# Four RMS norms that spread their sums with one product, in a two-block transformer kernel

## The chip, the cores and the metric

The kernel runs on one core of a Trainium2 chip, in one launch. The metric is the time of one execution in microseconds (us) of the device; the time before is the median of three runs. Engines are named as in the profile: PE is TensorE's products, PEld its weight loads, DVE is VectorE, ACT ScalarE, POOL GpSimd, SP SyncE (which issues the loads of weights).

## The reference

512 tokens of width 1024 pass a first block (two layers: a mixer, then cross attention to a memory of 256 rows) and a second block (pooling, latent attention, memory attention, a gated merge, then a mixture of 32 experts). What matters here are the norms:

```python
def rmsnorm(x, g):
    xf = x.astype(jnp.float32)
    y = xf * lax.rsqrt(jnp.mean(xf * xf, axis=-1, keepdims=True) + EPS)
    return (y * g.astype(jnp.float32)).astype(x.dtype)
...
        x = x + memory_cross_attention(rmsnorm(x, c_norm[i]), rmsnorm(mem, c_mem_norm[i]),
                                       c_wq[i], c_wkv[i], c_wo[i])
    return rmsnorm(x, final_norm)
```

Both layers of the first block norm the same `mem`, with different gains. The first block ends with a norm (gain `final_norm`), and the second begins with another one on its result (`mix_norm_g`), so two norms follow each other directly.

## The kernel before, in words

Activations lie transposed: features on the 128 partitions in 8 tiles (`KT`), the 512 tokens along the free dimension (`T`). A norm therefore sums over partitions and tiles. Every weight product is made in fp32r from high and low parts: `three` (with `tile`, 24 products for one output tile of 8 x 3) multiplies high by high, high by low, low by high. Weights come in units of 128x1024 through a ring of three buffers: SP loads one, ACT makes its high part (L572, `highs_through`, due once the unit three before it has been used), POOL its low part (L537). Output tiles go round four PSUM banks `G`; a bank is free again once DVE has emptied it (`evac`). Each engine runs a list written out by hand, in the order of the code; waits are semaphores.

The norm's factor is applied after the product: the inputs carry only the gain, and DVE multiplies each emptied tile by `RB`, the inverse root of each token's mean square, the same on all partitions (`scaled`, L1027). A norm runs so: ACT squares each tile (`norm_tile`, L585) and makes its high part (L587), DVE makes the low part (L988) and adds the squares up in `sumsq` (L993, L996). Then PE sums over the partitions with four column products of `sumsq` against a column of ones (`norm_cols`, into `O[:, 0:4]`: tokens on partitions now). ACT takes the root (`norm_root`, L592), DVE inverts it (`norm_cols` of DVE, L1003) and scales four 128x128 identity pieces with it (L1005, into `sq`), PE multiplies ones by this diagonal (`norm_bc`, into `TR`, the value of every token on all partitions), and DVE copies it to `RB` (`norm_bc` of DVE, L1014).

The norms in order: "e", "m0" (memory, 256 columns), "c0", "o", "m1" (memory again), "c1", "fm", "kvd", "qd", "m2", "ffn", "f2". Those the change touches:

- "c0" and "c1" (`cross`): columns after the third k tile, spreading after the fifth. `RB` is used from the q tiles on, which come after eight k tiles and the v tiles.
- "o": columns after the first conv tile, spreading after the second.
- "m1": squares and sums of the memory tiles on ACT and DVE (`mem_norm`, `mem_tiles`), columns and spreading inside the projection `o_out` (`project` with `beside`, `residual` with `beside`). Until `RBm` is there, the residual's own tiles are held back.
- "fm", the last norm of the first block and the first of the second in one: two sums are kept (`sumsq` of x squared and `sumsq_f`, of x times the gain squared). Eight columns after tile kvd0; a root (L765), an inverse `rcf` (L1359), the second sum scaled by it (L1360, L1361), a second root (L767) and inverse (L1363, L1364); two diagonals (L1366, L1368), two spreading products after tile kvd1, two copies (L1374 to `RB`, L1375 to `RBf`).

After "fm" DVE goes on in this order: `scaled` kvd0 and kvd1 with their norm tiles, `cosq` and `sinq` (L1381, L1382), `norm_cols` of "kvd", the rotation of kr (L1053, L1056, L1388), `scaled` qd0, the copy of RBk, qd1 and qd2 with their norm tiles. PE's order is kvd0, kvd1, kr, qd0, columns of "kvd", qd1, spreading of "kvd", qd2, uv0, columns of "qd", uk0, spreading of "qd". ACT makes the high part of the next unit between its norm tiles (`unit_done`).

Of the kernel before, what the change touches and what calls it, by code (L numbers as in the profile page):

```python
# [110 lines left out]
def build(nc, stream, x_in, mem_in, mem2_in, vectors, tables, decay, window, causal, pool_edge, positions, ident_in,  # L111
          router_w, router_b, iota_in, slot_in, before_in, w_gu, w_dn, out):
    ctx = ExitStack()
    with ctx:
# [25 lines left out]
        rcf = sb("rcf", [P, 4])  # L140
        rcq = sb("rcq", [P, 4])
        fm_ss = sb("fm_ss", [P, 4])
# [9 lines left out]
        sb("line_b", [P, HALF_LINE])  # L152
# [142 lines left out]
        NB, BC = {}, {}  # L295
        tiles = splits = 0
        for i, (name, n, w, split) in enumerate(NORMS):
            NB[name] = (i, tiles, splits, n, w, split)
            BC[name] = i - (1 if name == "f2" else 0)
            tiles += n  # L300
            splits += split

# [50 lines left out]
        sumsq_f, diag_f = U[:, 7, :], U[:, 6, :]  # L353
# [206 lines left out]
        def _(act):  # L560
# [17 lines left out]
            def norm_tile(name, f, src, gain, dst, ready):  # L578
                i, base, sbase, n, w, split = NB[name]
                act.wait_ge(*ready)  # L580
                if base + f >= 2:
                    act.wait_ge(ssq, base + f - 1)
                if f == 0 and i > 0:
                    act.wait_ge(bc_full, BC[name])
                nc.scalar.activation(sq[:, (base + f) % 2, 0:w], src, ACT.Square).then_inc(xsq, 1)  # L585
                if split:
                    nc.scalar.activation(dst, src, ACT.Identity, scale=gain).then_inc(xhi, 1)  # L587

            def norm_root(name, width):
                i, _, _, n, w, _ = NB[name]  # L590
# [100 lines left out]
            def mem_norm(name, raw, landed_sem, gain, beside):  # L691
# [4 lines left out]
                norm_root(name, D)  # L696
                unit_done(beside, 2)
                act.wait_ge(rb_ready, NB[name][0] + 1)
# [39 lines left out]
            norm_root("o", D)  # L738
# [12 lines left out]
            i, tile0 = NB["fm"][0], NB["fm"][1]  # L751
            for f in range(KT):
# [5 lines left out]
                if f == 0:  # L758
                    act.wait_ge(bc_full, i)
# [4 lines left out]
            act.wait_ge(col_full, i + 1)  # L764
# [175 lines left out]
            def final(again, added):  # L940
                i, base = NB["f2"][0], NB["f2"][1] - 1 + again * SUMMED
# [7 lines left out]
                act.wait_ge(col_full, i + 1 + again)  # L949
# [18 lines left out]
        def _(dve):  # L968
# [15 lines left out]
            def norm_tile(name, f, src, gain, hi, lo):  # L984
                i, base, sbase, n, w, split = NB[name]
                if split:
                    dve.wait_ge(xhi, sbase + f + 1)
                    nc.vector.scalar_tensor_tensor(lo, src, gain, hi, ALU.mult, ALU.subtract).then_inc(xlo, 1)  # L988
                dve.wait_ge(xsq, base + f + 1)
                if f == 0:  # L990
                    if i:
                        dve.wait_ge(col_full, i)
# [6 lines left out]
            def norm_cols(name, dst):  # L999

                i, _, _, n, w, _ = NB[name]
                dve.wait_ge(col_root, i + 1)
# [8 lines left out]
            def norm_bc(name, dst):  # L1011
                i, w = BC[name], NB[name][4]
                dve.wait_ge(bc_full, i + 1)
                nc.vector.tensor_copy(dst[:, 0:w], TR[:, 0:w]).then_inc(rb_ready, 1)  # L1014
                dve.wait_ge(rb_ready, i + 1)

# [297 lines left out]
            norm_end("o", rc, RB)  # L1314
# [19 lines left out]
            residual("o_out", "c1", "c_norm1", beside="m1")  # L1334
# [5 lines left out]
            i, tile0, split0 = NB["fm"][0:3]  # L1340
            for f in range(KT):
# [6 lines left out]
                for e, total in enumerate((sumsq[:, :], sumsq_f)):  # L1348
                    dve.wait_ge(xsq, tile0 + 2 * f + e + 1)
                    if f == 0:  # L1350
                        if e == 0:
                            dve.wait_ge(col_full, i)
# [9 lines left out]
            dve.wait_ge(col_root, i + 1)  # L1362
            do(nc.vector.reciprocal(rc[:, :], root[:, :]))  # L1363
            do(nc.vector.tensor_tensor(rc[:, :], rc[:, :], rcf[:, :], ALU.mult))  # L1364
            for t in range(TT):
                note(nc.vector.tensor_scalar(sq[:, 0, t * P:(t + 1) * P], ident[:, :], rc[:, t:t + 1], None, ALU.mult))  # L1366
            for t in range(TT):
                ins = nc.vector.tensor_scalar(diag_f[:, t * P:(t + 1) * P], ident[:, :], rcf[:, t:t + 1], None,  # L1368
                                              ALU.mult)
                if t < TT - 1:  # L1370
                    note(ins)
            ins.then_inc(diag, 1)
            dve.wait_ge(bc_full, i + 1)
            note(nc.vector.tensor_copy(RB[:, :], TR[:, :]))  # L1374
# [1289 lines left out]
```

## Time and profile before

| what | value |
|---|---|
| median of 3 runs | 1624.59 us (1622.58 to 1625.92) |
| profiled execution | 1624.31 us |
| its span, first to last instruction | 1622.5 us |
| PE busy | 1584.3 us, 98% of the span, 7432 products |
| PEld, DVE, ACT, POOL busy | 1203.4, 840.6, 583.8, 547.1 us |
| granted TensorE clock, mean | 0.991 of full speed |

The page gives, for one execution, each engine's busy time; the chain that ended last, followed back from the last instruction; and groups of instructions with the idle time ahead of them. The trace can be asked for the instructions of a stretch in order of time. In such an answer a line has the start in us from the span's start, the duration, engine, line, operation, out<-in, shape and count; a group that is merged begins at its first. Matmuls are pipelined: their starts tell the pace, their durations overlap. A product in fp32 (not fp32r) is issued as two.

### The profile page before, as it was taken

To read this page: it belongs to the slowest core of one execution; us is meant where nothing else is said; L and a number is where in the kernel's file an instruction comes from. 1 tells how busy PE (TensorE), PEld (TensorE's weight loads), DVE (VectorE), ACT (ScalarE), POOL (GpSimd) and SP (SyncE) were. 2 spreads that over 40 slices of the span, in tenths; PEclk is the share of its full clock that TensorE was granted. 3 is DMA by queue.
4 is the path that set the end of the run, shared out by engine and by line. 5 is a ranking of instruction groups with operands and counts; after the bars stand their busy time and mean duration, and the time that the engine had idled before them with its cause. 6 is when DMAs were issued, how large, how long until landed. Compare 5 with 4: busy or idle time off the path is not lost.

```text
span 1622.5 us, 20099 instructions
## 1 busy us (share of the span) xinstructions
PE 1584.3 (98%) x7432; PEld 1203.4 (74%) x7432; DVE 840.6 (52%) x1456; ACT 583.8 (36%) x963; POOL 547.1 (34%) x239
## 2 busy tenths in 40 slices
PE   7999989999999999999999999999999999999997
PEld 5888769886888888987887767888877885444543
DVE  6447586135645557354668686344243644433434
ACT  4127454334322225325533343343243333112213
POOL 4441226731444444851433124455424410000000
PEclk9999999999999999999999999999999989999998
DMA  5331224522223233531223013334312449999991
GB/s 188 96 99 40 78 78 130 163 85 71 92 91 101 95 96 99 168 118 41 79 78 91 27 52 97 100 125 128 97 52 92 153 179 368 417 423 422 421 418 68
DMA packets 52787, 235.94 MB, mean 145 GB/s; under 512 B 6240, under 2 KB 7136, under 8 KB 48096
## 3 DMA queue, kind: packets, MB, share of 16 engines
q1 hardware_dynamic: 48960, 222.60, 38.9%
q0 software_dynamic: 2016, 7.34, 1.1%
q10 hardware_dynamic: 1728, 4.87, 0.9%
q8 instruction: 55, 0.90, 0.2%
q14 instruction: 28, 0.23, 0.0%
HBM read 230.59 MB, written 4.19 MB: 145 GB/s over the span
## 4 chain that ended last, share of the span: by engine, by line
PE 90%; DVE 5%; ACT 2%; issue 1%; DMA 0%; SPq 0%; DVEq 0%; ACTq 0%
PE G L1804 69%; PE O L1804 7%; PE S L1804 6%; PE TR L1804 4%; PE TR L1914 2%; PE G L2376 1%; DVE sq L1056 1%; DMA w_ring<-in_stream_dram 0%; ACT hi_ring L572 0%; DVE U L1027 0%; DVE arena L1205 0%; DVE sumsq L1126 0%; DVE arena L1200 0%; DVE arena L1426 0%; DVE U L1781 0%
## 5 line engine op out<-in xcount | busy, mean ns | idle before, releaser
L537 POOL TENSOR_TENSOR lo_ring<-w_ring,hi_ring 128x1024 fp32r<-128x1024 f32 x219 | 533.4, 2437 | 775.2 <-ACT hi_ring L572 774.8
L572 ACT ACTIVATE hi_ring<-w_ring 128x1024 fp32r<-128x1024 f32 x219 | 231.2, 1058 | 577.8 <-PE G L1804 573.7
L1804 PE MATMUL G<-xa_hi,hi_ring 128*128 128x512 f32 x928 | 375.6, 405 | 9.8 <-DVE xa_lo L1118 9.6
L1804 PE MATMUL G<-xa_hi,lo_ring 128*128 128x512 f32 x928 | 362.4, 391 | 0.0
L1804 PE MATMUL G<-xa_lo,hi_ring 128*128 128x512 f32 x928 | 362.1, 390 | 0.0
L1804 PEld LDWEIGHTS G<-xa_hi,hi_ring 128*128 128x128 f32 x928 | 174.9, 188 | 48.2 <-issue 12.2
L1804 PEld LDWEIGHTS G<-xa_lo,hi_ring 128*128 128x128 f32 x928 | 174.9, 188 | 38.0 <-issue 2.6
L1804 PEld LDWEIGHTS G<-xa_hi,lo_ring 128*128 128x128 f32 x928 | 174.6, 188 | 37.1
L1804 PE MATMUL G<-yb_hi,hi_ring 128*128 128x512 f32 x388 | 153.4, 395 | 4.1 <-ACT arena L670 2.2
L1804 PE MATMUL G<-yb_hi,lo_ring 128*128 128x512 f32 x388 | 151.1, 389 | 0.0
L1804 PE MATMUL G<-yb_lo,hi_ring 128*128 128x512 f32 x388 | 151.0, 389 | 0.0
L1027 DVE TENSOR_TENSOR arena<-G,RB 128x512 f32<-128x512 f32 x77 | 52.6, 689 | 156.4 <-PE G L1804 155.8
L548 POOL DMA_INDIRECT ex_raw<-token_rows,arena x14 | 13.3, 947 | 227.0 <-DVE arena L1676 224.8
L1804 PEld LDWEIGHTS G<-yb_hi,hi_ring 128*128 128x128 f32 x388 | 72.8, 188 | 20.6 <-issue 5.2
L1804 PEld LDWEIGHTS G<-yb_lo,hi_ring 128*128 128x128 f32 x388 | 72.8, 188 | 15.9 <-issue 1.0
L1804 PEld LDWEIGHTS G<-yb_hi,lo_ring 128*128 128x128 f32 x388 | 72.8, 188 | 15.3
L1804 PE MATMUL G<-cm_hi,hi_ring 128*128 128x256 f32 (+1 forms) x212 | 69.3, 327 | 0.1
L996 DVE TENSOR_TENSOR sumsq<-sumsq,sq 128x512 f32<-128x512 f32 (+1 forms) x51 | 65.6, 1286 | 1.9 <-ACT sq L585 1.9
L1804 PE MATMUL G<-cm_hi,lo_ring 128*128 128x256 f32 (+1 forms) x212 | 65.6, 309 | 0.0
L1804 PE MATMUL G<-cm_lo,hi_ring 128*128 128x256 f32 (+1 forms) x212 | 65.6, 309 | 0.0
L1804 PE MATMUL G<-ex_rings,U 128*64 128x512 f32 x160 | 57.9, 595 | 0.0
L1804 PE MATMUL TR<-ex_rings,U 128*64 128x512 f32 x128 | 56.6, 595 | 0.0
(350 smaller groups left out, 2503.0 us busy)
## 6 DMA issues: line engine op xcount, KB each, us to landing
w_ring<-in_stream_dram SPq DMA_DIRECT2D x219, 512.0 KB, 3.5
arena<-in_w_gu_dram SPq DMA_DIRECT2D x16, 2048.0 KB, 11.5
ex_rings<-in_w_dn_dram SPq DMA_DIRECT2D x40, 512.0 KB, 15.2
ex_low<-in_w_gu_dram SPq DMA_DIRECT2D x8, 2048.0 KB, 17.8
ex_rings<-in_w_gu_dram SPq DMA_DIRECT2D x8, 2048.0 KB, 15.4
arena<-in_w_dn_dram SPq DMA_DIRECT2D x16, 512.0 KB, 13.7
sq<-in_w_dn_dram SPq DMA_DIRECT2D x8, 512.0 KB, 17.3
X<-in_x_in_dram SPq DMA_DIRECT2D x8, 256.0 KB, 5.8
```

The source lines that it names most:

```text
L537: nc.gpsimd.tensor_tensor(lo_ring[:, s, :], w_ring[:, s, :], hi_ring[:, s, :], ALU.subtract).then_inc(low, 1)
L548: nc.gpsimd.indirect_dma_start(slot_rows[p], None, token_rows, where).then_inc(rows_land[p], 16)
L572: nc.scalar.activation(hi_ring[:, m % RING, :], w_ring[:, m % RING, :], ACT.Copy).then_inc(high, 1)
L996: nc.vector.tensor_tensor(sumsq[:, 0:w], sumsq[:, 0:w], sq[:, (base + f) % 2, 0:w], ALU.add).then_inc(ssq, 1)
L1027: nc.vector.tensor_tensor(dst, G[:, a % BANKS, 0:w], by, ALU.mult).then_inc(evac, done)
L1056: ins = nc.vector.tensor_tensor(part[other, 1, :], bank[r, :], sin[r, :], ALU.mult)
L1804: return nc.tensor.matmul(*args, **kw)
L1914: ins = nc.tensor.transpose(TR[:, b * P:(b + 1) * P], prob(probs, u, b * P, (b + 1) * P), ident[:, :])
L2376: ins = nc.tensor.transpose(G[:, f // 2, c:c + P], slot_rows[p][:, f * P:(f + 1) * P], ident[:, :])
```

## The change

The norms "c0", "o", "c1" and "fm" are marked `wide`: one product of ones (128x128) with `sumsq` (128x512) puts each token's sum on all partitions at once, ACT takes the root of 128x512, and DVE inverts it in place. Columns, diagonal and the copy fall away for them. In "c0" and "c1" the product stands where the columns stood, after the third k tile; in "o" after the first conv tile; in "fm" two products stand after tile kvd0, where the columns stood, and none after kvd1. "m1" has no squares, sums, columns or spreading: `rcm` and `RBm` of "m0" are used again, since the memory is the same. The semaphore counts are kept in tables of their own (`COL`, `BC`, `ROOT`, `DIAG`, `SUMS_READ`), since not every norm signals each of them any more.

```diff
@@ the norms @@
-        NORMS = [("e", KT, T, KT), ("m0", KT, MEM, KT), ("c0", KT, T, KT), ("o", KT, T, KT), ("m1", KT, MEM, KT),
-                 ("c1", KT, T, KT), ("fm", 2 * KT, T, KT), ("kvd", 2, T, 2), ("qd", 3, T, 3),
-                 ("m2", KT, MEM, KT), ("ffn", KT, T, 0), ("f2", KT, T, 0)]
+        NORMS = [("e", KT, T, KT, "cols"), ("m0", KT, MEM, KT, "cols"), ("c0", KT, T, KT, "wide"),
+                 ("o", KT, T, KT, "wide"), ("m1", 0, MEM, KT, ""), ("c1", KT, T, KT, "wide"),
+                 ("fm", 2 * KT, T, KT, "wide"), ("kvd", 2, T, 2, "cols"), ("qd", 3, T, 3, "cols"),
+                 ("m2", KT, MEM, KT, "cols"), ("ffn", KT, T, 0, "cols only"), ("f2", KT, T, 0, "cols")]
@@ tiles @@
-        rcf = sb("rcf", [P, 4])
-        fm_ss = sb("fm_ss", [P, 4])
-        sb("line_b", [P, HALF_LINE])
+        sb("line_b", [P, HALF_LINE + 8])
@@ ACT @@
+            def wide_root(name):
+                act.wait_ge(bc_full, BC[name] + 1)
+                nc.scalar.activation(RB[:, :], TR[:, :], ACT.Sqrt, bias=eps[:, :], scale=1.0 / D).then_inc(col_root, 1)
...
                         if name[0] == "k" and j == 2:
-                            norm_root(norm, D)
+                            wide_root(norm)
...
             residual("o0", "o", "o_norm")
-            norm_root("o", D)
+            wide_root("o")
...
             unit_done("kvd", 0)
-            act.wait_ge(col_full, i + 1)
-            nc.scalar.activation(root[:, :], O[:, 0:4], ACT.Sqrt, bias=eps[:, :], scale=1.0 / D).then_inc(fm_root, 1)
+            act.wait_ge(bc_full, BC["fm"] + 1)
+            nc.scalar.activation(RBf, TR[:, :], ACT.Sqrt, bias=eps[:, :], scale=1.0 / D).then_inc(fm_root, 1)
             act.wait_ge(fm_mid, 1)
-            nc.scalar.activation(root[:, :], fm_ss[:, :], ACT.Sqrt, bias=eps[:, :], scale=1.0 / D).then_inc(col_root, 1)
+            nc.scalar.activation(RB[:, :], RB[:, :], ACT.Sqrt, bias=eps[:, :], scale=1.0 / D).then_inc(col_root, 1)
             unit_done("kvd", 1)
@@ DVE @@
+            def wide_inverse(name):
+                dve.wait_ge(col_root, ROOT[name] + 1)
+                nc.vector.reciprocal(RB[:, :], RB[:, :]).then_inc(rb_ready, 1)
+                dve.wait_ge(rb_ready, BC[name] + 1)
...
             def cross(i, norm):
                 for j in range(KT):
                     scaled(ACC0[f"k{i}"] + j, xk[:, j, :], RBm[:, :], MEM)
-                    if j == 3:
-                        norm_cols(norm, rc)
                     if j == 4:
-                        norm_bc(norm, RB)
+                        wide_inverse(norm)
...
             residual("o0", "o", "o_norm")
-            norm_end("o", rc, RB)
+            wide_inverse("o")
...
-            residual("o_out", "c1", "c_norm1", beside="m1")
+            residual("o_out", "c1", "c_norm1")
...
             dve.wait_ge(fm_root, 1)
-            do(nc.vector.reciprocal(rcf[:, :], root[:, :]))
-            do(nc.vector.tensor_tensor(fm_ss[:, :], O[:, 4:8], rcf[:, :], ALU.mult))
-            nc.vector.tensor_tensor(fm_ss[:, :], fm_ss[:, :], rcf[:, :], ALU.mult).then_inc(fm_mid, 1)
-            dve.wait_ge(col_root, i + 1)
-            do(nc.vector.reciprocal(rc[:, :], root[:, :]))
-            do(nc.vector.tensor_tensor(rc[:, :], rc[:, :], rcf[:, :], ALU.mult))
...
-            note(nc.vector.tensor_copy(RB[:, :], TR[:, :]))
-            nc.vector.tensor_copy(RBf, O[:, :]).then_inc(rb_ready, 1)
-            settle()
-            dve.wait_ge(rb_ready, i + 1)
+            do(nc.vector.reciprocal(RBf, RBf))
+            do(nc.vector.tensor_tensor(RB[:, :], O[:, :], RBf, ALU.mult))
+            nc.vector.tensor_tensor(RB[:, :], RB[:, :], RBf, ALU.mult).then_inc(fm_mid, 1)
+            dve.wait_ge(col_root, ROOT["fm"] + 1)
+            do(nc.vector.reciprocal(RB[:, :], RB[:, :]))
+            nc.vector.tensor_tensor(RB[:, :], RB[:, :], RBf, ALU.mult).then_inc(rb_ready, 1)
+            dve.wait_ge(rb_ready, BC["fm"] + 1)
@@ PE @@
-            def norm(name):
-                norm_cols(name)
-                norm_bc(name)
+            def norm_wide(name):
+                base, _, n, _, _ = NB[name]
+                pe.wait_ge(ssq, base + n)
+                mm(TR[:, :], ones[:, :], sumsq[:, :], start=True, stop=True).then_inc(bc_full, 1)
...
                     if j == 2:
-                        norm_cols(norm_name)
-                    if j == 4:
-                        norm_bc(norm_name)
+                        norm_wide(norm_name)
...
             tile("conv", 0, xa_hi, xa_lo, ready=low_ready("o"))
-            norm_cols("o")
-            tile("conv", 1, xa_hi, xa_lo)
-            norm_bc("o")
-            for i in range(2, 32):
+            norm_wide("o")
+            for i in range(1, 32):
                 tile("conv", i, xa_hi, xa_lo)
-            project("o_out", yb_hi, yb_lo, YL["conv"], y_low, KT - 1, beside="m1")
+            project("o_out", yb_hi, yb_lo, YL["conv"], y_low, KT - 1)
...
             tile("kvd", 0, xa_hi, xa_lo, ready=low_ready("fm"))
-            i, tile0 = NB["fm"][0], NB["fm"][1]
-            pe.wait_ge(ssq, tile0 + 2 * KT)
-            for e, total in enumerate((sumsq[:, :], sumsq_f)):
-                for t in range(TT):
-                    ins = mm(O[:, 4 * e + t:4 * e + t + 1], total[:, t * P:(t + 1) * P], ones[:, 0:1],
-                             start=True, stop=True)
-            ins.then_inc(col_full, 1)
+            pe.wait_ge(ssq, NB["fm"][0] + 2 * KT)
+            mm(TR[:, :], ones[:, :], sumsq[:, :], start=True, stop=True)
+            mm(O[:, :], ones[:, :], sumsq_f, start=True, stop=True).then_inc(bc_full, 1)
             tile("kvd", 1, xa_hi, xa_lo)
-            pe.wait_ge(diag, i + 1)
-            mm(TR[:, :], ones[:, :], sq[:, 0, :], start=True, stop=True)
-            mm(O[:, :], ones[:, :], diag_f, start=True, stop=True).then_inc(bc_full, 1)
             tile("kr", 0, xa_hi, xa_lo)
```

Squares and sums of a norm are skipped where its count of tiles is 0 ("m1"), on ACT and DVE alike; ACT's `mem_norm` then neither takes a root nor waits for `rb_ready`.

## Rows read from the trace of the kernel before

**Rows 1.** The page: PE's busy time, and the chain that ended last by engine.

```profile
PE 1584.3 (98%) x7432; PEld 1203.4 (74%) x7432; DVE 840.6 (52%) x1456; ACT 583.8 (36%) x963; POOL 547.1 (34%) x239
...
PE 90%; DVE 5%; ACT 2%; issue 1%; DMA 0%; SPq 0%; DVEq 0%; ACTq 0%
```

**Rows 2.** Busy us by stretch: PE, PEld, DVE, ACT, POOL; PEclk, DMA share, GB/s.

```profile
1280.00:1622.00 342.00, 328.17 (x1618) 184.97 (x1616) 150.89 (x295) 89.31 (x142) 25.38 (x19) 0.96 0.82 333
```

**Rows 3.** The chain that ended last from 800 to 870: start, us, what.

```profile
799.94 17.91 PE G L1804 x79
...
827.07 10.94 PE G L1804 x48
838.10 1.06 ACT hi_ring L572
...
856.64 0.69 DVE sumsq L996
857.37 1.05 PE O L1804 x8
```

**Rows 4.** PE in order of time around norm "o".

```profile
432.16 0.95 PE L1804 MATMUL O<-ones,sumsq 128*128 128x1 f32 x8
...
438.53 1.02 PE L1804 MATMUL TR<-sq,ones 128*128 128x512 f32 x2
```

**Rows 5.** PE in order of time around norm "m1".

```profile
618.96 0.50 PE L1804 MATMUL O<-ones,sumsq 128*128 128x1 f32 x4
...
624.91 0.59 PE L1804 MATMUL TR<-sq,ones 128*128 128x256 f32 x2
...
625.81 0.40 PE L1804 MATMUL G<-yb_hi,lo_ring 128*128 128x512 f32 x1
```

**Rows 6.** PE in order of time around norm "fm" and the kvd columns.

```profile
817.85 1.05 PE L1804 MATMUL O<-ones,sumsq 128*128 128x1 f32 x8
...
825.19 1.02 PE L1804 MATMUL TR<-sq,ones 128*128 128x512 f32 x2
...
837.84 0.95 PE L1804 MATMUL O<-ones,sumsq 128*128 128x1 f32 x8
```

**Rows 7.** A root over 128x512 (durations min/median/max) and two reciprocals in a row.

```profile
L670 ACT ACTIVATE arena<-G,eps x2: 687/687/687, 188.3 to 212.3; 128x512 f32<-128x512 f32 x2
...
213.03 3.37 DVE L1200 RECIPROCAL arena<-arena 128x256 f32<-128x256 f32 x2 [1.31 <-ACT arena L670]
```

**Rows 8.** ACT and DVE in order of time in and after norm "fm".

```profile
820.31 0.27 ACT L765 ACTIVATE root<-O,eps 128x4 f32<-128x4 f32 x1
...
822.26 0.87 DVE L1366 TENSOR_SCALAR sq<-ident,rc 128x128 f32<-128x128 f32 x4
...
827.72 0.68 DVE L1375 COPY arena<-O 128x512 f32<-128x512 f32 x1
828.49 0.69 DVE L1027 TENSOR_TENSOR U<-G,RB 128x512 f32<-128x512 f32 x1
...
834.76 2.89 DVE L1381 TENSOR_TENSOR arena<-arena,RB 128x512 f32<-128x512 f32 x1
837.58 0.68 DVE L1382 TENSOR_TENSOR arena<-arena,RB 128x512 f32<-128x512 f32 x1
839.41 0.18 DVE L1003 RECIPROCAL rck<-root 128x4 f32<-128x4 f32 x1 [1.15 <-ACT root L592]
839.62 2.69 DVE L1005 TENSOR_SCALAR sq<-ident,rck 128x128 f32<-128x128 f32 x4
```

**Rows 9.** POOL and DVE in order of time: ops that meet each other.

```profile
630.97 5.43 POOL L537 TENSOR_TENSOR lo_ring<-w_ring,hi_ring 128x1024 fp32r<-128x1024 f32 x2 [7.78 <-ACT hi_ring L572]
...
634.07 2.88 DVE L996 TENSOR_TENSOR sumsq<-sumsq,sq 128x512 f32<-128x512 f32 x1
...
834.49 2.62 POOL L537 TENSOR_TENSOR lo_ring<-w_ring,hi_ring 128x1024 fp32r<-128x1024 f32 x1 [5.51 <-ACT hi_ring L572]
839.24 2.40 POOL L537 TENSOR_TENSOR lo_ring<-w_ring,hi_ring 128x1024 fp32r<-128x1024 f32 x1 [2.13 <-ACT hi_ring L572]
```

More of the change, by code:

```diff
@@ L289, in build @@
         stored = sem("out_stored")
-        NORMS = [("e", KT, T, KT), ("m0", KT, MEM, KT), ("c0", KT, T, KT), ("o", KT, T, KT), ("m1", KT, MEM, KT),
-                 ("c1", KT, T, KT), ("fm", 2 * KT, T, KT), ("kvd", 2, T, 2), ("qd", 3, T, 3),
-                 ("m2", KT, MEM, KT), ("ffn", KT, T, 0), ("f2", KT, T, 0)]
[L295 to L299, printed above, removed]
+        NORMS = [("e", KT, T, KT, "cols"), ("m0", KT, MEM, KT, "cols"), ("c0", KT, T, KT, "wide"),
+                 ("o", KT, T, KT, "wide"), ("m1", 0, MEM, KT, ""), ("c1", KT, T, KT, "wide"),
+                 ("fm", 2 * KT, T, KT, "wide"), ("kvd", 2, T, 2, "cols"), ("qd", 3, T, 3, "cols"),
+                 ("m2", KT, MEM, KT, "cols"), ("ffn", KT, T, 0, "cols only"), ("f2", KT, T, 0, "cols")]
+        NB, COL, BC, ROOT, DIAG, SUMS_READ = {}, {}, {}, {}, {}, {}
+        tiles = splits = cols = bcs = roots = diags = 0
+        before_it = None
+        for name, n, w, split, kind in NORMS:
+            NB[name] = (tiles, splits, n, w, split)
+            COL[name], BC[name], ROOT[name], DIAG[name] = cols, bcs, roots, diags
+            SUMS_READ[name] = before_it
             tiles += n
             splits += split
+            if kind:
+                cols += kind != "wide"
+                bcs += kind != "cols only"
+                diags += kind == "cols"
+                roots += 1
+                before_it = (bc_full, bcs) if kind == "wide" else (col_full, cols)
         YB = {}
@@ L352, in build @@
         RBf = A(4224, T)
-        sumsq_f, diag_f = U[:, 7, :], U[:, 6, :]
+        sumsq_f = U[:, 7, :]
         qrope = A(4992, 2, T)
@@ L578, in norm_tile @@
             def norm_tile(name, f, src, gain, dst, ready):
-                i, base, sbase, n, w, split = NB[name]
+                base, sbase, n, w, split = NB[name]
                 act.wait_ge(*ready)
[L581 to L585, printed above, removed]
+                if n:
+                    if base + f >= 2:
+                        act.wait_ge(ssq, base + f - 1)
+                    if f == 0 and BC[name]:
+                        act.wait_ge(bc_full, BC[name])
+                    nc.scalar.activation(sq[:, (base + f) % 2, 0:w], src, ACT.Square).then_inc(xsq, 1)
                 if split:
@@ L695, in mem_norm @@
                 unit_done(beside, 1)
-                norm_root(name, D)
+                if NB[name][2]:
+                    norm_root(name, D)
                 unit_done(beside, 2)
-                act.wait_ge(rb_ready, NB[name][0] + 1)
+                if NB[name][2]:
+                    act.wait_ge(rb_ready, BC[name] + 1)
             def residual(stage, norm, gain, split=True):
@@ L940, in final @@
             def final(again, added):
-                i, base = NB["f2"][0], NB["f2"][1] - 1 + again * SUMMED
+                base = NB["f2"][0] - 1 + again * SUMMED
                 for f in range(KT):
@@ L948, in final @@
                     nc.scalar.activation(sq[:, f % 2, :], X[:, f, :], ACT.Square).then_inc(xsq, 1)
-                act.wait_ge(col_full, i + 1 + again)
+                act.wait_ge(col_full, COL["f2"] + 1 + again)
                 nc.scalar.activation(root[:, :], O[:, 0:4], ACT.Sqrt, bias=eps[:, :],
@@ L988, in norm_tile @@
                     nc.vector.scalar_tensor_tensor(lo, src, gain, hi, ALU.mult, ALU.subtract).then_inc(xlo, 1)
+                if not n:
+                    return
                 dve.wait_ge(xsq, base + f + 1)
                 if f == 0:
-                    if i:
-                        dve.wait_ge(col_full, i)
+                    if SUMS_READ[name]:
+                        dve.wait_ge(*SUMS_READ[name])
                     nc.vector.tensor_copy(sumsq[:, 0:w], sq[:, (base + f) % 2, 0:w]).then_inc(ssq, 1)
@@ L1011, in norm_bc @@
             def norm_bc(name, dst):
-                i, w = BC[name], NB[name][4]
+                i, w = BC[name], NB[name][3]
                 dve.wait_ge(bc_full, i + 1)
@@ L1702, in square_sum @@
             def square_sum(again, f):
-                base = NB["f2"][1] - 1 + again * SUMMED
-                dve.wait_ge(xsq, NB["f2"][1] + again * KT + f + 1)
+                base = NB["f2"][0] - 1 + again * SUMMED
+                dve.wait_ge(xsq, NB["f2"][0] + again * KT + f + 1)
                 if f == 0:
-                    dve.wait_ge(col_full, NB["f2"][0] + again)
+                    dve.wait_ge(col_full, COL["f2"] + again)
                     nc.vector.tensor_copy(sumsq[:, :], sq[:, 0, :]).then_inc(ssq, 1)
@@ L1771, in final @@
             def final(again):
-                i = NB["f2"][0]
-                dve.wait_ge(col_root, i + 1 + again)
+                dve.wait_ge(col_root, ROOT["f2"] + 1 + again)
                 do(nc.vector.reciprocal(rc[:, :], root[:, :]))
@@ L1888, in norm_cols @@
             def norm_cols(name):
-                i, base, _, n, w, _ = NB[name]
+                base, _, n, w, _ = NB[name]
                 pe.wait_ge(ssq, base + n)
@@ L2115, in _ @@
             base = SU["mla"]
-            pe.wait_ge(rb_ready, NB["kvd"][0] + 1)
+            pe.wait_ge(rb_ready, BC["kvd"] + 1)
             wide("uv0", 1, TT, lat_hi, lat_lo, 3, 2)
@@ L2227, in _ @@
                 tile("xq", j, xa_hi, xa_lo)
-            pe.wait_ge(rb_ready, NB["m2"][0] + 1)
+            pe.wait_ge(rb_ready, BC["m2"] + 1)
             base = SU["x2"]
@@ L2294, in _ @@
             pe.wait_ge(raw_up, 4)
-            base = NB["ffn"][1]
+            base = NB["ffn"][0]
             for part in range(2):
@@ L2466, in final @@
             def final(again):
-                base = NB["f2"][1]
+                base = NB["f2"][0]
                 def columns(part, first, last):
```

37 lines of the change are left out of this document (14 added, 23 removed).

## The prediction, made before the change was run

> **What bounds the kernel now.** I read the page first: TensorE (PE) is busy for 98% of the span and carries 90% of the chain that ended last [rows 1]. A shorter PE program is therefore a shorter kernel, unless another engine's chain takes over. The last 340 us move 333 GB/s with the DMA engines busy for 82% [rows 2]; its loads start on events that PE's own progress sets, so time saved before it passes through whole.
>
> Then I read the chain of waits around the double norm "fm", a stretch in which PE does not set the pace alone. 79 products take 17.91 us, a pace of 0.2267 us each, and 48 more run without a break up to about 838; but from 838.10 to 857.37 the chain is ACT and VectorE (DVE), and PE waits at its end for the last sum of "qd" [rows 3]. So a saving on PE ahead of 838 counts only as far as this DVE chain comes earlier too.
>
> **The change, part by part.** The times are those of the trace of before; what is saved upstream moves all of them alike.
>
> PE, norms "c0", "c1" and "o": four column products each go. In "o" they start at 432.16, and after the 24 products of one tile the spreading product starts at 438.53 [rows 4]: 6.37 less 24 x 0.2267 (5.44) leaves 0.93 us. "c0" and "c1" issue the same four, 0.93 each. The spreading product itself stays: it has the same shape, ones as weights and 512 columns moving, and only sits where the columns were.
>
> PE, norm "m1": two columns (618.96 to 624.91 less 5.44: 0.51) and the spreading product of 256 columns (the third product after it starts at 625.81 instead of 625.36: 0.45) go: 0.96 [rows 5].
>
> PE, "fm": eight columns and two spreading products become two spreading products. Columns: 825.19 less 817.85 less 5.44 is 1.90. The pair: 837.84 less 825.19 less 48 x 0.2267 (10.88) is 1.77, so 0.89 for one [rows 6]. The pair now comes right behind tile kvd0 at 817.85, and qd0 ends at 817.85 + 1.77 + 72 x 0.2267 = 835.94 instead of 837.84.
>
> So PE alone loses 3 x 0.93 + 0.96 = 3.75 us outside "fm" and 1.90 in it, 5.65 together.
>
> DVE and ACT, "c0", "c1", "o": a root over 128x512 for one over 128x4 (0.69 against 0.27 us [rows 7, 8]), and a reciprocal over 128x512 for a small one, four diagonal pieces and a copy. Two reciprocals over 128x256 in a row take 3.37 [rows 7], so I take 3.36 for one over 128x512; the fixed part of a second instruction, at most the 0.18 of a reciprocal of 4 columns [rows 8], could go, and nothing in the trace runs longer per column. I cost all this at nothing. What hides it: in "c0" and "c1" RB is first read by the q tiles, after the v tiles, and four PSUM banks let the next k tile be emptied some 1 us late. If that cover were gone, PE would stop for about that 1 us. In "o" RB is ready at about 432.16 + 1.02 + 0.69 + 3.36 = 437.3, where the old spreading product only starts at 438.53 [rows 4]. The product there still waits for the same sum as the columns did.
>
> "m1": eight squares on ACT and eight sums on DVE go; ACT no longer waits for RBm before the residual. PE waits for none of them now, so nothing comes back, and rcm and RBm of "m0" are simply kept. The 8 floats by which line_b grows make up for rcf and fm_ss. No DMA or queue moves.
>
> **The chain in "fm"** is what decides. New, in order:
> 1. The pair of products ends at 817.85 + 0.86 + 1.02 = 819.73. ACT's table load ends at 820.31, where the old root starts [rows 8]. Root over 128x512 from PSUM, 0.69 [rows 7]: 821.0.
> 2. DVE: reciprocal 3.36 (824.4), product with a PSUM operand 0.69 (825.1), product from SBUF 0.68 (825.8); GpSimd (POOL) is idle then.
> 3. ACT: second root, by the same row at most 0.69: 826.5. Only then can ACT convert the weights of the tile that kvd1 freed, 1.06 us, and POOL's op of 2.40 [rows 9] runs from about 827.55 to 829.95.
> 4. DVE: second reciprocal to 829.9, then the last product, which meets the end of that POOL op: about 830.6. Before, the two copies ended at 828.4 and the first scaled tile began at 828.49 [rows 8]. RB comes 2.15 late, and PE runs 1.90 early.
>
> From there the scaling, the latent norms and their sums shift by 2.15. PE, which reaches the kvd columns at 835.94, waits for the kvd sum until 837.0. The product cosq, 2.89 long at 834.76, is shown beside a POOL op of 2.62 at 834.49 and should be beside it again [rows 8, 9]. But the second ACT conversion now needs no wait (qd0 is long done), so the next POOL op is queued right behind the first. The trace has that case: two POOL ops back to back take 5.43 from 630.97, one DVE op gets in between them, and the DVE product started at 634.07 takes 2.88 [rows 9]. So sinq, 0.68 before [rows 8], waits out the second POOL op: that ends at 836.64 + 5.43 + 0.2 = 842.3, and sinq at 842.85. Reciprocal and four diagonal pieces (0.87 without POOL, 2.69 beside it [rows 8]) follow: 843.95 instead of 842.31. Everything that DVE does up to the last qd sum comes 1.65 late, so PE passes 857.37 at 859.0. It loses the 1.90 and 1.65 more.
>
> What that weighs by rule: the Trainium skill, SBUF — State Buffer, section "SBUF: two separate sides", says that DVE ops with two SBUF inputs and GpSimd ops take a shared port pair as an exclusive lock, and the one that starts first blocks the other for its whole length. By it sinq waits as above. A rule that speaks against the sizes here: the Trainium skill, VectorE: DVE Perf Modes, section "First, the fixed hardware budget", gives the reciprocal a repeat count of 8, which with that page's clock of 0.96 GHz would be an estimate of 4.27 us for 512 columns. The trace disagrees: two of 256 take 3.37 [rows 7]. By it the sum would be -0.3 instead of -2.1.
>
> **Sum.** -3.75 + 1.65 = -2.1 us. The profiled execution took 1624.31 (span 1622.5 and 1.8 around it), so 1622.2; it lies 0.28 below the median of the three runs, 1624.59, from which the same difference gives 1622.5. I say 1622.4.
>
> **Rivals.** What a measurement of this kernel can tell from no change is about 0.2%, 3.25 us.
> - **Sinq gets in first.** If DVE keeps its turn between the two POOL ops, the diagonal ends at about 842.4 and "fm" costs 0.1: -3.65, 1620.7. For: it takes only a few tenths more between two ops of POOL. Against: the pair at 630.97 [rows 9]. Chance 0.23.
> - **"fm" hidden whole.** If PE had slack for all of the longer chain, the full 5.65 shows: 1618.7. For: three tiles, 16.3 us, lie between the pair and the kvd columns. Against: the chain from 838.10 is already without slack [rows 3]. Chance 0.08.
> - **One more collision.** The last product of step 4 starts at the very end of a POOL op; should that op begin a little later (ACT's conversion is tied to step 3), it takes 2.9 instead of 0.7, and "fm" costs 3.85: +0.1, 1624.4. The change then saves nothing, against what its text says. Two reciprocals that are 0.9 us longer each than their row says would end near the same place (-0.3); [rows 7] speaks against it. Chance for both, 0.14. (The second is what the Trainium skill's page VectorE: DVE Perf Modes, section "First, the fixed hardware budget", would give.)
> - **Slower: the long reciprocal holds POOL.** Place: k4 of "c0" and "c1", and "fm". If a reciprocal of 3.36 shut POOL out, the weights' low parts, one 2.40 op for each 2.88 us of a k tile, would come up to 2.9 late against some 1.9 us of slack: 1.1 each. In "fm" the same lock puts the POOL op behind the second reciprocal and the last product behind it: 3.85. That is -3.75 + 2.2 + 3.85 = +2.3, 1626.6. It decides as soon as POOL's ops wait longer than the ring's slack. Against: the reciprocal at 839.41 takes its usual 0.18 in the middle of a POOL op, where the diagonal behind it is held [rows 8]. No row shows the large one beside POOL. Chance 0.07.
>
> My forecast has 0.48. Range: 1619.6 to 1625.6 leaves out the hidden case and the slower one, and allows about 1 us beyond the two nearer rivals for the runs' own spread. Faster by over 0.2% needs 3.25 us: the hidden case, two thirds of the first rival and some 0.07 of my own tail, 0.30. Slower by over 0.2% takes a slower case that comes out worse, 0.05. Within: 0.65.
>
> **What would show it.** Right: 22 column products and one spreading product fewer; RECIPROCAL 128x512 five times at 3.3 to 3.4 us; a PE wait of about 1 us before the kvd columns and of some tenths before the kvd spreading product; sinq at 2.9; the stretch from kvd0's end to the qd columns (39.52 us before) at about 41.2. Wrong: that stretch under 40 us (first or second rival), a last "fm" product of over 2 us (third), POOL ops stretched to over 3 us in the k tiles (fourth), or a PE wait in c0, c1 or o that was not there.

## The result, and the profile after

The changed kernel takes 1643.62 us (median of 4 runs, 1642.60 to 1643.78), the kernel before 1624.79 beside it: a ratio of 1.0115, with a 95% interval of 1.0102 to 1.0128. That is 19 us slower, where the prediction said 2 us faster and its range ended at 1625.6. The profiled execution has a span of 1641.8 us against 1622.5.

The page of the changed kernel, busy time and chain; [rows 1] are the same lines of before:

```profile
PE 1599.0 (97%) x7386; PEld 1196.3 (73%) x7386; DVE 852.0 (52%) x1419; ACT 583.0 (36%) x954; POOL 547.3 (33%) x239
...
PE 89%; DVE 7%; issue 2%; ACT 2%; DMA 0%; SPq 0%; DVEq 0%; ACTq 0%
```

PE issues 46 products fewer (the 22 columns and one spreading product of the forecast, each issued as two) and is busy 14.7 us longer. The same page's groups of weight products (count, then busy us and mean ns of one) say which:

```profile
L1810 PE MATMUL G<-xa_hi,hi_ring 128*128 128x512 f32 x928 | 380.7, 410 | 9.3 <-DVE xa_lo L1139 9.3
L1810 PE MATMUL G<-xa_lo,hi_ring 128*128 128x512 f32 x928 | 367.5, 396 | 0.0
...
L1810 PE MATMUL G<-yb_hi,lo_ring 128*128 128x512 f32 x388 | 151.7, 391 | 0.0
```

And the same groups on the page of before:

```profile
L1804 PE MATMUL G<-xa_hi,hi_ring 128*128 128x512 f32 x928 | 375.6, 405 | 9.8 <-DVE xa_lo L1118 9.6
...
L1804 PE MATMUL G<-xa_lo,hi_ring 128*128 128x512 f32 x928 | 362.1, 390 | 0.0
...
L1804 PE MATMUL G<-yb_hi,lo_ring 128*128 128x512 f32 x388 | 151.1, 389 | 0.0
```

`xa` is the normed input of a projection, `yb` the result of a mixer or of attention on its way into the next projection, and `cm` the normed memory and later the latents; each is a tile pair of high and low parts. The 2784 products with `xa` as the input have become slower, though no instruction among them was touched; those with `yb` as the input, with weights from the same rings, hardly. A product's duration is modelled, so I read the pace, that is, the time from one product's start to the next, in a stretch that holds nothing but such products. Of three products that follow each other one is high weights by `xa_lo`; its group from 500 to 600 us, in the kernel before and in the changed one (count, min/median/max ns, first and last start):

```profile
L1804 PE MATMUL G<-xa_lo,hi_ring x147: 389/389/389, 500.2 to 599.5; 128*128 128x512 f32 x147
```

```profile
L1810 PE MATMUL G<-xa_lo,hi_ring x144: 393/395/397, 499.7 to 599.8; 128*128 128x512 f32 x144
```

Before, 99.3 us for 146 steps of three: 0.2267 us for a product. After, 100.1 for 143: 0.2333. Every single one in this stretch is slow (least 393 ns, where the most before was 389), so it is no wait here and there. Taken over all 928 steps, that is an estimate of 928 x (0.7000 - 0.6801) = 18.4 us. The products with `cm` as the input went both ways: by their groups' busy time 2.5 us more for those of 512 columns, 2.0 less for those of 256. Where the ring is the moving operand and `cm` or `xa` lies in the array, the groups gained 1.8 and 0.5 us.

The wide products, PE in order of time (in brackets the idle time ahead and what ended it):

```profile
274.69 1.12 PE L1810 MATMUL TR<-sumsq,ones 128*128 128x512 f32 x2 [1.44 <-DVE sumsq L1012]
...
437.73 1.02 PE L1810 MATMUL TR<-sumsq,ones 128*128 128x512 f32 x2
...
665.72 1.13 PE L1810 MATMUL TR<-sumsq,ones 128*128 128x512 f32 x2 [1.43 <-DVE sumsq L1012]
...
828.50 1.12 PE L1810 MATMUL TR<-sumsq,ones 128*128 128x512 f32 x2
...
869.67 1.05 PE L1810 MATMUL O<-ones,sumsq 128*128 128x1 f32 x8 [1.13 <-DVE sumsq L1012]
```

In "c0" and "c1" PE waits 1.44 and 1.43 us for the last sum, which it did not before. So the account is 18.4 + 2.9 of waits - 2.1 of the forecast = 19.2, against 19.3 between the two spans. It names the two large terms; that it meets the difference to a tenth is luck. Its first term is read from 100 us (by busy time the three `xa` groups gained 15.4), and the smaller changes of the other groups are left out.

**"fm" itself went as forecast.** The chain that ended last in the changed kernel, behind the end of kvd0:

```profile
831.12 0.70 ACT arena L779
...
831.84 3.36 DVE arena L1378
...
835.23 0.70 DVE RB L1379
...
835.96 0.70 DVE RB L1380
...
836.68 0.73 ACT RB L781
...
837.44 3.36 DVE RB L1382
...
840.82 0.70 DVE RB L1383
```

and DVE and POOL behind it in order of time, to be held against [rows 8, 9]:

```profile
847.55 5.40 POOL L544 TENSOR_TENSOR lo_ring<-w_ring,hi_ring 128x1024 fp32r<-128x1024 f32 x2 [6.73 <-ACT hi_ring L579]
847.82 2.87 DVE L1388 TENSOR_TENSOR arena<-arena,RB 128x512 f32<-128x512 f32 x1
...
850.62 2.88 DVE L1389 TENSOR_TENSOR arena<-arena,RB 128x512 f32<-128x512 f32 x1
...
853.75 0.87 DVE L1021 TENSOR_SCALAR sq<-ident,rck 128x128 f32<-128x128 f32 x4
```

Two reciprocals of 3.36, the last product 0.70 without a collision, two POOL ops back to back, `sinq` at 2.88, the diagonal without POOL at 0.87. From 828.50 to 869.67 is 41.17 us, where the prediction named about 41.2. All of that is right, and it weighs 2 us in a kernel that lost 19.

What did move is where the tiles lie in SBUF. Tiles are laid one behind the other in the order of their declaration. The offsets below are those of the two built programs, not of a trace. In them each small tile takes 32 bytes of a partition, although `rcf` and `fm_ss` need 16. Two of them go (64 bytes), `line_b` grows by 32, and the tiles behind it lie 32 bytes lower:

```
byte offset in a partition    before     changed
xa_hi                          32896       32896
xa_lo                          49280       49280
hi_ring                       171392      171360
lo_ring                       183680      183648
yb_lo                         195968      195936
yb_hi                         212352      212320
```

The weights (rings) and `yb` moved together; `xa` and `cm` stayed. That fits which products became slow, and was the theory for the runs.

### The profile page after: what moved, and what is told of

The parts are those of the page before. It is cut to its first block, busy times and chain, and to the rows that moved or that the text cites. A ratio compares the mean times of both kernels' runs of the same rounds, so it can differ in the third digit from the quotient of the medians.

```text
span 1641.8 us, 19943 instructions
## 1 busy us (share of the span) xinstructions
PE 1599.0 (97%) x7386; PEld 1196.3 (73%) x7386; DVE 852.0 (52%) x1419; ACT 583.0 (36%) x954; POOL 547.3 (33%) x239
## 4 chain that ended last, share of the span: by engine, by line
PE 89%; DVE 7%; issue 2%; ACT 2%; DMA 0%; SPq 0%; DVEq 0%; ACTq 0%
PE G L1810 69%; PE O L1810 7%; PE S L1810 6%; PE TR L1810 4%; PE TR L1921 2%; DVE sumsq L1012 1%; PE G L2372 1%; DVE sq L1077 1%; DVE U L1048 0%; DMA w_ring<-in_stream_dram 0%; ACT hi_ring L579 0%; DVE sumsq L1147 0%; DVE arena L1433 0%; DVE U L1787 0%; DVE arena L1226 0%
## 5 line engine op out<-in xcount | busy, mean ns | idle before, releaser
L1810 PE MATMUL G<-xa_hi,hi_ring 128*128 128x512 f32 x928 | 380.7, 410 | 9.3 <-DVE xa_lo L1139 9.3
L1810 PE MATMUL G<-xa_lo,hi_ring 128*128 128x512 f32 x928 | 367.5, 396 | 0.0
L1810 PE MATMUL G<-xa_hi,lo_ring 128*128 128x512 f32 x928 | 367.3, 396 | 0.0
```

The costliest lines, as they stand in the source:

```text
L1810: return nc.tensor.matmul(*args, **kw)
```

## The experiments

### The changed kernel with the rings put back

```diff
-        sb("line_b", [P, HALF_LINE + 8])
+        sb("line_b", [P, HALF_LINE + 16])
```

> The changed kernel whole, with line_b eight floats longer still, so that the three weight rings and the two yb tiles lie at the byte offsets of the kernel before (w_ring at 159104 in place of 159072). No instruction differs from the changed kernel. Placement theory (the 19 us are TensorE's pace: products whose weights come from a ring moved by 32 bytes and whose inputs did not move take 0.234 us in place of 0.227): the median gap of xa products returns to 0.227 us, and the time is the blind forecast's sum, 1624.6 - 2.1 = 1622.5 us, with a stretch from kvd0's end to qd's columns of some 41.2 us. Rival (the new instructions themselves slow TensorE: the wide products, the long reciprocals, another order of the two engines' access to SBUF): the gap stays at 0.234 and the time at 1643 to 1644 us.

Measured: 1624.2 us (11 runs) against 1626.06 for the kernel before on the same chip (23 runs), ratio 0.9994 [0.9985, 1.0002], that is 1.0 us faster with an interval of -2.4 to +0.3. (Here and below the ratio with its interval is not the quotient of the two medians; those are 1.9 us apart.) The pace is back, 100.0 us for 147 steps, 0.2268:

```profile
L1810 PE MATMUL G<-xa_lo,hi_ring x148: 389/389/389, 500.0 to 600.0; 128*128 128x512 f32 x148
```

Eight floats that nothing reads are worth 1.2% of this kernel; the instructions of the change are not what slowed it. Since the placement is now the one of before, its trace can be laid beside that one term by term. PE at the sums of c0, o, c1 and fm, at the kvd columns and at the qd columns:

```profile
271.49 1.02 PE L1810 MATMUL TR<-sumsq,ones 128*128 128x512 f32 x2
...
432.95 1.02 PE L1810 MATMUL TR<-sumsq,ones 128*128 128x512 f32 x2
...
654.61 1.02 PE L1810 MATMUL TR<-sumsq,ones 128*128 128x512 f32 x2
...
815.80 1.12 PE L1810 MATMUL TR<-sumsq,ones 128*128 128x512 f32 x2
...
835.20 1.02 PE L1810 MATMUL O<-ones,sumsq 128*128 128x1 f32 x8 [1.07 <-DVE sumsq L1012]
...
856.79 1.05 PE L1810 MATMUL O<-ones,sumsq 128*128 128x1 f32 x8 [1.14 <-DVE sumsq L1012]
```

The columns of c0 and c1 in the kernel before (those of o and fm are in [rows 4, 6]):

```profile
269.81 0.95 PE L1804 MATMUL O<-ones,sumsq 128*128 128x1 f32 x8
...
655.78 0.95 PE L1804 MATMUL O<-ones,sumsq 128*128 128x1 f32 x8
```

From c0's sum to o's: 162.35 before, 161.46 here, so c0's term is 0.89. From o to c1: 223.62 and 221.66, 1.96 for o and m1. From c1 to fm: 162.07 and 161.19, 0.88. Together 3.73, forecast 3.75. From fm to the qd columns: 39.52 and 40.99, a loss of 1.47, forecast 1.65; PE's wait ahead of the kvd columns, 1.07, is the one forecast at about 1 us. The waits of 1.44 and 1.43 ahead of c0 and c1 are gone. By these stretches the change saves 3.73 - 1.47 = 2.26 us. The two spans (1622.5 and 1619.1) lie further apart; the rest arises ahead of c0 and behind the qd columns, where nothing was changed.

### The kernel before with the rings moved as in the changed one

```diff
-        sb("line_b", [P, HALF_LINE])
+        sb("line_b", [P, HALF_LINE - 8])
```

> The kernel before with nothing changed but line_b, eight floats shorter, so that the rings and the yb tiles lie 32 bytes lower, as in the changed kernel. Placement theory: the gap of xa and cm products goes from 0.227 to 0.234 us, that of yb products stays, and the time rises by 19 to 22 us to 1644 to 1646 us. Rival (the new instructions): 1624.6 us, as before.

Measured: 1646.67 us (4 runs), ratio 1.0134 [1.0119, 1.0149], 21.8 us slower (20.6 between the medians). `xa` at 0.2333 us (99.4 for 142 steps), `yb` unchanged (27.9 us for 41 steps, 0.2268), and PE waits before c0's and c1's columns, though no wide sum is there:

```profile
L1804 PE MATMUL G<-xa_lo,hi_ring x143: 393/395/397, 500.2 to 599.6; 128*128 128x512 f32 x143
...
L1804 PE MATMUL G<-yb_lo,hi_ring x42: 389/389/390, 395.6 to 423.5; 128*128 128x512 f32 x42
...
274.68 1.05 PE L1804 MATMUL O<-ones,sumsq 128*128 128x1 f32 x8 [1.43 <-DVE sumsq L996]
...
668.51 1.05 PE L1804 MATMUL O<-ones,sumsq 128*128 128x1 f32 x8 [1.44 <-DVE sumsq L996]
```

18.4 + 2.9 is 21.3, and its span is 1643.9, 21.4 over the one of before; the same reserve holds as for the first account. So these two waits come with the placement as well. What they come from shows in "c0". The last sum on DVE in the kernel before, which began together with a POOL op at 268.33:

```profile
268.33 0.68 DVE L996 TENSOR_TENSOR sumsq<-sumsq,sq 128x512 f32<-128x512 f32 x1
```

and the same sum in the changed kernel, behind a POOL op that began 0.09 us earlier:

```profile
271.69 2.39 POOL L544 TENSOR_TENSOR lo_ring<-w_ring,hi_ring 128x1024 fp32r<-128x1024 f32 x1 [0.39 <-ACT hi_ring L579]
271.78 2.86 DVE L1012 TENSOR_TENSOR sumsq<-sumsq,sq 128x512 f32<-128x512 f32 x1
```

In "c1" it is the same (654.29 and 0.68 before, 662.81 and 2.85 after). That the slower pace is what shifts the two engines against each other is read from the traces; no run here changed the shift alone.

### The changed kernel with "fm" as it was, at the placement of before

```diff
-                 ("fm", 2 * KT, T, KT, "wide"), ("kvd", 2, T, 2, "cols"), ("qd", 3, T, 3, "cols"),
+                 ("fm", 2 * KT, T, KT, "fm"), ("kvd", 2, T, 2, "cols"), ("qd", 3, T, 3, "cols"),
...
+        rcf = sb("rcf", [P, 4])
+        fm_ss = sb("fm_ss", [P, 4])
...
-        sb("line_b", [P, HALF_LINE + 8])
+        sb("line_b", [P, HALF_LINE])
...
-            mm(TR[:, :], ones[:, :], sumsq[:, :], start=True, stop=True)
-            mm(O[:, :], ones[:, :], sumsq_f, start=True, stop=True).then_inc(bc_full, 1)
+            for e, total in enumerate((sumsq[:, :], sumsq_f)):
+                for t in range(TT):
+                    ins = mm(O[:, 4 * e + t:4 * e + t + 1], total[:, t * P:(t + 1) * P], ones[:, 0:1],
+                             start=True, stop=True)
+            ins.then_inc(col_full, 1)
```

(and the roots, inverses, diagonals and copies of the kernel before on ACT and DVE).

> The changed kernel with the norm fm put back as it was (columns, diagonals, rcf and fm_ss), so four wide sums are down to three, and with every tile at its address of before. Forecast's terms: c0, c1, o and m1 save 0.93 x 3 + 0.96 = 3.75 us of TensorE and fm costs nothing: 1624.6 - 3.75 = 1620.9 us, 1.65 under the changed kernel at the same placement. Rival A (c0's wide sum waits for VectorE, as it did for 1.2 us in the changed kernel): 1622.0 us. Rival B (fm's new chain costs nothing, so its products' saving stands): this kernel is 1.9 us slower than the changed kernel at the same placement.

Measured: 1622.93 us, the median of 11 runs, ratio 0.9981 [0.9972, 0.9990] to the kernel before: 3.1 us faster, -4.5 to -1.6. A twelfth run took 4139.96 us; it is left out, and its cause stays open (with it the median is 1623.34). This kernel is faster than the one before, clear of noise. PE at the sums of o and c1, at fm's columns and at the qd columns:

```profile
436.00 1.02 PE L1824 MATMUL TR<-sumsq,ones 128*128 128x512 f32 x2
...
657.70 1.02 PE L1824 MATMUL TR<-sumsq,ones 128*128 128x512 f32 x2
...
818.89 1.05 PE L1824 MATMUL O<-ones,sumsq 128*128 128x1 f32 x8
...
858.42 1.05 PE L1824 MATMUL O<-ones,sumsq 128*128 128x1 f32 x8 [1.16 <-DVE sumsq L1014]
```

The last stretch is 39.53 us, as before the change, and 1.46 less than with fm wide. From o to c1, 221.70; from c1 to fm, 161.19: the same savings as in the first run. The rivals of this run fall by the trace: c0's wide product starts at 274.52 without a wait, and fm's saving does not stand. The medians of the two kernels at the same placement lie 1.3 us apart and their ratios 2.1, around the 1.65 forecast, but their intervals overlap: for the size of fm's term the traces speak, not the times.

### Which offset counts: the inputs moved instead

```diff
+        sb("pad_inputs", [P, 8])
         xa_hi = sb("xa_hi", [P, KT, T], F32R)
...
-        sb("line_b", [P, HALF_LINE])
+        sb("line_b", [P, HALF_LINE - 8])
```

> The kernel before with a pad of 32 bytes ahead of xa_hi, so that all tiles from xa_hi to the small ones lie 32 bytes higher, and line_b eight floats shorter, so that rings and yb tiles stay where they were. Relative theory (what counts is the offset between a product's weights and its moving input): xa and cm products take 0.234 us, yb products 0.227, and the time is some 1644 us, as with the rings moved down. Absolute theory (what counts is where the ring alone lies): the gaps are 0.227 and the time 1624.6 us. Third reading (what counts is where the moving input alone lies): slow here too, but then the changed kernel, whose xa did not move, is not explained.

Measured: 1648.06 us (4 runs), ratio 1.0140 [1.0125, 1.0155]; the pace is that of the second run, and PE again waits 1.46 and 1.44 us ahead of the columns of c0 and c1:

```profile
L1805 PE MATMUL G<-xa_lo,hi_ring x143: 393/395/397, 500.1 to 599.5; 128*128 128x512 f32 x143
```

The ring lies where it lay in the fast kernel, and `xa` is slow: its place alone is not what counts.

### Everything moved, and yb alone

First the pad ahead of `xa_hi` alone, so that inputs and rings rise together:

> The kernel before with a pad of 32 bytes ahead of xa_hi and nothing else, so that xa, cm, U, arena, rings and yb all lie 32 bytes higher and only X stays. Relative theory: every gap as before (0.227), some 1625 us. Absolute theory (a multiple of 64 bytes is wanted for each operand by itself): xa and yb gaps 0.234 us or more, 1645 to 1655 us.

Measured: 1625.53 us beside 1627.29 (one run each), pace 100.0 us for 147 steps:

```profile
L1805 PE MATMUL G<-xa_lo,hi_ring x148: 389/389/389, 499.7 to 599.7; 128*128 128x512 f32 x148
```

The inputs lie where they lay in the experiment before this one, and their products are fast here: their place alone does not decide either.

Then `yb` alone:

```diff
+        early("pad_yb", [P, 8])
         yb_lo = early("yb_lo", [P, KT, T], F32R)
...
+        sb("pad_ex", [P, 8])
         ex_low = sb("ex_low", [P, KT * T])
```

> The kernel before with the two yb tiles alone 32 bytes higher (and the expert tiles over them). Relative theory: now the yb products are the slow ones, 0.234 us, and xa products stay at 0.227; 3 x 388 yb products at 7 ns more are 8.1 us, so some 1633 us. Rival (the slow pace belongs to xa and cm tiles, whatever the yb tiles do): 0.227 in both and 1625 us.

Measured: 1637.17 us beside 1627.29 (one run each). Now `xa` is fast and `yb` slow, 28.0 us for 40 steps, 0.2333:

```profile
L1806 PE MATMUL G<-xa_lo,hi_ring x148: 388/389/390, 499.8 to 599.8; 128*128 128x512 f32 x148
...
L1806 PE MATMUL G<-yb_lo,hi_ring x41: 393/394/397, 395.9 to 423.9; 128*128 128x512 f32 x41
```

The pace hangs on the distance between a product's weights and its moving input. The time is 4 us above the 1633 expected. Most of that seems to be the granted clock's, read from traces and not tested: the columns of c0 are already 4.58 us late, and in the last of these runs, which has the same dips of the clock and no slow pace, 3.55 (see there).

### The period of it

In the kernel before, rings and `yb` are raised by 64 bytes (`line_b` at `HALF_LINE + 16`), by 128 (`HALF_LINE + 32`) and by 256 (`HALF_LINE + 64`). In one run more `hi_ring` is raised by 16 bytes and `lo_ring` by 48, within longer tiles, and `yb` by 64.

> The kernel before with line_b 16 floats longer: rings and yb tiles 64 bytes higher (hi_ring at 171456), inputs xa and cm where they were. If the offset between a product's two operands counts modulo 64 bytes, the xa gap is 0.227 us and the time some 1625 us; if modulo 128, the gap is 0.234 and the time some 1645 us. A third outcome, a gap under 0.227, would mean that the placement of before is not the best one.

> The kernel before with hi_ring 16 bytes and lo_ring 48 bytes higher within longer tiles, and the yb tiles 64 bytes higher. If any offset that is no multiple of 64 is slow: xa and yb gaps 0.234 us, 1624.6 + 20 + 8 = some 1653 us. If only bit 5 of the offset counts, the products on hi_ring (16 bytes) keep 0.227 and those on lo_ring (48 bytes) take 0.234. If 16 bytes is a third case, another gap.

> The kernel before with line_b 32 floats longer: rings and yb tiles 128 bytes higher (hi_ring at 171520), 138624 bytes above xa_hi, an odd multiple of 128 where it was a multiple of 256. Modulo 128: the xa gap is 0.227 us and the time some 1625 us. Modulo 256 (the offsets 64 and 96 would be slow under both): the gap is 0.234 and the time some 1645 us.

> The kernel before with line_b 64 floats longer: rings and yb tiles 256 bytes higher (hi_ring at 171648), 138752 bytes above xa_hi, a multiple of 512. Of the offsets tried, 32, 64, 96 (32 down) and 128 bytes away from the placement of before were slow. Modulo 256: the xa gap is 0.227 us again and the time some 1625 us. If the fast placement of before is a single lucky one (modulo 512 or more, or an address of its own): 0.234 and some 1643 us.

Measured, one run each: 64 up, 1644.41 us (beside 1627.29); 16 and 48 up, 1649.72 (1627.29); 128 up, 1641.78 (1624.22); 256 up, 1627.96 (1621.66). The same group in this order:

```profile
L1804 PE MATMUL G<-xa_lo,hi_ring x144: 393/396/399, 499.9 to 600.0; 128*128 128x512 f32 x144
```

```profile
L1807 PE MATMUL G<-xa_lo,hi_ring x143: 397/397/397, 500.1 to 599.5; 128*128 128x512 f32 x143
```

```profile
L1804 PE MATMUL G<-xa_lo,hi_ring x144: 390/393/404, 499.9 to 599.6; 128*128 128x512 f32 x144
```

```profile
L1804 PE MATMUL G<-xa_lo,hi_ring x148: 389/389/389, 499.7 to 599.6; 128*128 128x512 f32 x148
```

That is 0.2333, 0.2333, 0.2324 and 0.2265 us. In the second of these, a step of three holds two products on `hi_ring` and one on `lo_ring`, so its pace is the mean over both distances. My readings "modulo 64" and "modulo 128" fell, each by an experiment (64 up, 128 up) in which it had forecast the pace of before. Of the distances tried, only those that are multiples of 256 bytes are fast: before and "everything up" (hi_ring less xa_hi is 138496, 541 x 256), 256 up (542 x 256), and `yb` (yb_hi less hi_ring is 40960, 160 x 256) wherever it was fast. Distances of 64, 128 and 224 bytes beyond a multiple, and 16 and 48 together, are slow; others were not tried.

The last one is fast in pace and yet its span is 3.7 us above that of the kernel before (1626.2 against 1622.5), and its time 6.3 above the run beside it. Two stretches of the two executions (length, PE busy, granted clock, DMA share, GB/s), before and then 256 up:

```profile
0.00:60.00 60.00, 48.49 (x206) 1.00 0.48 160
...
210.00:222.00 12.00, 9.16 (x37) 1.00 0.40 132
```

```profile
0.00:60.00 60.00, 47.92 (x197) 0.97 0.47 154
...
210.00:222.00 12.00, 8.85 (x25) 0.72 0.37 131
```

A granted clock of 0.72 over 12 us is more than half of them at 1.2 in place of 2.4 GHz. In both stretches PE has pauses (it is busy for 8.85 of the 12 us), and behind them the clock fell in one execution and not in the other. The columns of c0 start at 273.36 us against 269.81, those of fm at 821.40 against 817.85: the same 3.55 both times, so nearly all of the 3.7 arises ahead of c0. The changed kernel with the rings put back has only the second of the two dips (1.00, then 0.72) and is late by 1.68 us at its c0 sum; the run with `yb` moved has both (0.97, then 0.72). That the clock makes the 3.55 fits these traces; no run set the clock by itself. This is why single times here are told apart by 20 us and not by 3, and why I read the paces.

## Why the prediction was wrong

- **The step that failed** is the sentence "The 8 floats by which line_b grows make up for rcf and fm_ss." It counted 4 + 4 floats against 8, where the built program gives each of the two tiles 32 bytes; the rings came to lie 32 bytes lower. And it put the placement of the tiles at nothing without a reason. The sum held PE's pace at 0.2267 us in every term, and no rival asked what would change it. A pace 3% slower in 2784 products is some 18.4 us, and two waits of 1.4 us come with it; putting 32 bytes back removes both.
- **PE's terms**: 3.75 forecast for c0, o, m1 and c1; 3.73 in the trace at equal placement. Right.
- **"fm"**: +1.65 forecast; +1.47 at equal placement, and 41.17 us against "about 41.2" in the changed kernel itself. The reciprocals (3.34 to 3.36), the collision of `sinq`, the diagonal beside no POOL op: right, each at its size. The estimate of 4.27 us for the reciprocal, which I had worked out from the repeat count in the Trainium skill, VectorE: DVE Perf Modes, section "First, the fixed hardware budget", does not hold here.
- **The net**: -2.1 forecast; -2.26 by the stretches of the traces at equal placement, -1.0 [-2.4, +0.3] by the times, whose interval holds the forecast and no change alike. In the traces the changed instructions do what the prediction said; the times cannot confirm it.
- **The rivals**: sinq gets in first, fm hidden whole and the collision of the last product did not come. The long reciprocal does not hold POOL: POOL ops beside it stay at 2.4 us. The slower side, which I gave 0.07 and some 2 us, came by a way that none of them named.
- **What the text named as signs**: "a PE wait in c0, c1 or o that was not there" did show, and by itself would have pointed at the wide sums. The second run shows it without a wide sum.

A POOL op of the changed kernel in "c0", and the reciprocal that was running when it began:

```profile
282.65 2.40 POOL L544 TENSOR_TENSOR lo_ring<-w_ring,hi_ring 128x1024 fp32r<-128x1024 f32 x1 [0.39 <-ACT hi_ring L579]
```

```profile
281.80 3.34 DVE L1035 RECIPROCAL RB<-RB 128x512 f32<-128x512 f32 x1
```

## What to carry to other kernels

If a changed kernel's time runs away evenly from its first microseconds on, ahead of the place of the edit, look at paces by operand pair rather than for a wait. A pad named like `line_b` that nothing reads is there for its size: treat its number as part of the tuning.

## What the runs showed of the hardware

- At full granted clock an fp32r product of 128x128 weights, loaded anew for each, with 512 moving columns follows the one before it after 0.2265 to 0.2268 us when the distance between the two operands' places is a multiple of 256 bytes, and after 0.2324 to 0.2333 at the other distances tried. Which tile is moved makes no difference: 0.2333 with the rings 32 bytes down, 0.2333 with the inputs 32 up, 0.2268 with both up. I had taken the pace for a constant of the shape.
- The Trainium skill, TensorE: Matmul & The Clock Gate, section "Step-by-step: what each phase is for", says that the streaming operand and the weight load have a read port each, so that loading the next weights takes nothing from the running product. Going by that alone, placement would change nothing; these traces disagree by 3%. Why the distance matters stays open: that every product of the stretch is slow, also while ACT and POOL write nothing into the ring, speaks for PE's own two reads against each other, but no run here took one of them away.
- Products of 256 columns on `cm` do not follow the pattern: in the changed kernel those on `cm` were busy 2.0 us less in all. This was not looked into further.
- The granted clock differs between executions of the same program: the 23 runs of the kernel before beside the first four experiments have means of 0.989 to 0.992 and take 1629.02 to 1623.06 us, the lower clock mostly with the longer time.
- A DVE sum of 128x512 with both inputs in SBUF took 0.68 us when it began together with a POOL op and 2.86 when it began 0.09 us behind one, which ran 2.39. A reciprocal of 128x512 took 3.34 beside a POOL op that kept its 2.40.
